# Forget gates and keys as two sigmoids, level products in a fourth bank beside the latent attention, and one accumulator per half for the latents' and heads' output projection

## The reference

```
for l in range(2):
    h = x @ w_in[l]            # hg_q, hg_f, hg_i, hg_gate (1024 each), mla_cq, mla_ckv, mla_kr, mla_gate, mem_q, mem_gate
    # recurrent heads (8 heads of 128)
    logf = log_sigmoid(hg_f) + log1p(lb * exp(-hg_f))      # f = lb + (1 - lb) * sigmoid(hg_f)
    k    = (1 - lb) * sigmoid(-hg_f)
    S_t  = diag(f_t) S_{t-1} + k_t v_t^T ;  o_t = S_t^T q_t         # v = hg_i
    y_hg = rmsnorm_per_head(o) * out_g * silu(hg_gate)
    # latent attention (8 heads of 64 + 32), causal softmax
    y_mla = attend(...) * silu(mla_gate)
    # memory attention (4 heads of 128)
    y_mem = attend(...) * silu(mem_gate)
    x = layernorm(4 ** 0.25 * x + concat(y_hg, y_mla, y_mem) @ w_out[l])
```

## Time and profile before

| | us |
|---|---|
| runs (3): lowest, median, highest | 1034.55, 1035.75, 1036.23 |
| the profiled execution: its time | 1040.25 |
| the profiled execution: its span | 1038.5 |
| TensorE busy in the span | 997.3 |
| VectorE busy | 690.4 |
| ScalarE busy | 605.7 |
| mean granted clock of TensorE | 0.980 |

### The profile page before, as it was taken

How to read it: one execution, slowest core, us unless ns; L and a number is a source line. 1 busy time by engine, 2 the same in 40 slices (tenths; PEclk the granted TensorE clock), 3 DMA queues, 4 the chain that set the end, 5 groups by cost and what they waited for, 6 DMA issues and landing times.

```text
span 1038.5 us, 18803 instructions
## 1 busy us (share of the span) xinstructions
PE 997.3 (96%) x8042; PEld 896.5 (86%) x8042; DVE 690.4 (66%) x917; ACT 605.7 (58%) x828; POOL 10.8 (1%) x14
## 2 busy tenths in 40 slices
PE   9999999999999999999999999896999999998967
PEld 7899887888989999988999998695799999977945
DVE  5775588875656887865565646983675556579645
ACT  7687567554465666554466768347355666682561
POOL 0000000000000000000000000100000000010000
PEclk9999999999999999999999999998999999998989
DMA  8852455477557556666554534434455555234411
GB/s 291 279 172 82 143 171 167 132 232 206 180 148 239 168 173 193 194 213 184 166 163 131 183 103 142 144 111 135 144 176 152 152 150 178 80 123 153 155 61 40
DMA packets 97283, 166.45 MB, mean 160 GB/s; under 512 B 6896, under 2 KB 32240, under 8 KB 96816
## 3 DMA queue, kind: packets, MB, share of 16 engines
q1 hardware_dynamic: 95792, 159.18, 48.8%
q0 software_dynamic: 976, 4.46, 1.3%
q10 hardware_dynamic: 432, 1.62, 0.4%
HBM read 164.19 MB, written 1.05 MB: 159 GB/s over the span
## 4 chain that ended last, share of the span: by engine, by line
PE 90%; ACT 4%; issue 3%; DVE 3%; DMA 1%; SPq 0%; DVEq 0%; ACTq 0%
PE proj L625 13%; PE proj L616 13%; PE proj L626 13%; PE proj L627 13%; PE proj L617 13%; PE proj L618 13%; PE mix L951 1%; PE mix L661 1%; PE mix L686 1%; PE mix L669 1%; ACT whi L1064 1%; PE mix L886 1%; DVE arena L1932 1%; DMA raw<-in_w_mem_kv 1%; PE mix L694 1%
## 5 line engine op out<-in xcount | busy, mean ns | idle before, releaser
L1526 DVE TENSOR_TENSOR wlo<-raw,whi 128x1024 fp32r<-128x1024 f32 (+2 forms) x304 | 355.2, 1198 | 162.1 <-ACT whi L1064 160.6
L1064 ACT ACTIVATE whi<-raw 128x1024 fp32r<-128x1024 f32 (+2 forms) x304 | 306.6, 1038 | 207.7 <-PE proj L627 90.5
L616 PE MATMUL proj<-act_hi,whi 128*128 128x256 f32 x1064 | 304.8, 287 | 2.8 <-ACT arena L1081 2.2
L617 PE MATMUL proj<-act_lo,whi 128*128 128x256 f32 x1064 | 301.7, 284 | 0.0
L618 PE MATMUL proj<-act_hi,wlo 128*128 128x256 f32 x1064 | 301.6, 284 | 0.0
L616 PEld LDWEIGHTS proj<-act_hi,whi 128*128 128x128 f32 x1064 | 203.9, 192 | 5.7 <-ACT arena L1081 3.1
L617 PEld LDWEIGHTS proj<-act_lo,whi 128*128 128x128 f32 x1064 | 203.9, 192 | 0.5
L618 PEld LDWEIGHTS proj<-act_hi,wlo 128*128 128x128 f32 x1064 | 204.0, 192 | 0.2
L625 PE MATMUL proj<-whi,y_hi 128*128 128x512 f32 (+1 forms) x340 | 138.1, 406 | 19.8 <-DVE X L2041 18.6
L626 PE MATMUL proj<-wlo,y_hi 128*128 128x512 f32 (+1 forms) x340 | 135.3, 398 | 0.0
L627 PE MATMUL proj<-whi,y_lo 128*128 128x512 f32 (+1 forms) x340 | 134.6, 396 | 0.0
(11 more groups left out here) (347 smaller groups left out, 1037.3 us busy)
## 6 DMA issues: line engine op xcount, KB each, us to landing
raw<-in_w_in SPq DMA_DIRECT2D x144, 512.0 KB, 4.5
raw<-in_w_up SPq DMA_DIRECT2D x88, 256.0 KB, 4.4
raw<-in_w_out SPq DMA_DIRECT2D x32, 512.0 KB, 4.6
raw<-in_w_down SPq DMA_DIRECT2D x22, 512.0 KB, 5.4
raw<-in_w_mem_k SPq DMA_DIRECT2D x8, 512.0 KB, 3.8
raw<-in_w_o SPq DMA_DIRECT2D x8, 512.0 KB, 3.9
raw<-in_w_mem_v SPq DMA_DIRECT2D x8, 512.0 KB, 3.5
raw<-in_w_mem_kv SPq DMA_DIRECT2D x7, 512.0 KB, 6.6
```

What stands on the lines that cost most here:

```text
L616: mm(o, wh[:, i, wc], hi[:, k0 + i, :], start=begin and j % 2 == 0, stop=False, skip_group_check=True)
L617: mm(o, wh[:, i, wc], lo[:, k0 + i, :], start=False, stop=False, skip_group_check=True)
L1064: fn(whi[c % SPLIT][:, 0:w], raw[c % SLOTS][:, 0:w], ACT.Copy).then_inc(s.w_hi, 1)
L1526: tt(wlo[c % SPLIT][:, 0:w], raw[c % SLOTS][:, 0:w], f32(whi[c % SPLIT][:, 0:w]), ALU.subtract).then_inc(s.w_lo, 1)
```

## The change

It has three parts. (1) ScalarE takes `FORGET` and `HKT` as sigmoids of hg_f and of -hg_f straight from the projection's bank; VectorE's forget arithmetic goes, the second layer scales in place. The keys and grown queries move to memory under `y_hi` and `y_lo`, `TOTAL` to a tile of its own. (2) The latent scores are packed into three banks of `mix` (`LATENT`), and levels 8 to 5 use the fourth, in turns with the latent attention's steps and with at least one projection piece between levels. (3) The two output projections of latents and heads become `heads0` and `heads1`, each with 6 pieces summed in one accumulator: the latents' two pieces first, then the heads' four. `mlaout0`, `mlaout1`, their two additions to X and `hgo` go; all four output pairs are in `mix`; `squares` writes the bank it read from, after `gated`. ScalarE and not VectorE copies the diagonal.

```diff
-    at = [name for name, _ in groups].index("hgg0")
-    groups[at:] = [("mlaout0", mlaout[0]), ("hgg0", hg["hgg0"]), ("hgg1", hg["hgg1"]), ("mlaout1", mlaout[1]), ("hgo", [])]
-    groups += [(f"hgout{c}", wide(out, c * 512)) for c in range(2)]
+    groups += [(f"heads{c}", wide(out, c * 512, row=1024, rows=512) + wide(out, c * 512)) for c in range(2)]
     if L + 1 < LAYERS:
...
 LEVELS = (8, 7, 6, 5, 4, 3, 2, 1, 0)
-LEVEL_BANK = {8: 1, 7: 2, 6: 3, 5: 0, 4: 1, 3: 2, 2: 3}
+LEVEL_BANK = {8: 3, 7: 3, 6: 3, 5: 3, 4: 2, 3: 1, 2: 3}
 GROWS = 7
 
 
...
-        if key[1] == "hgout0":
-            runs = [((key[0], f"hgout{c}"), b, e) for c, b, e in ((0, 0, 3), (1, 0, 1), (0, 3, 4), (1, 1, 4))]
+        if key[1] == "heads0":
+            runs = [((key[0], f"heads{c}"), b, e) for c, b, e in ((0, 0, 2), (1, 0, 2), (0, 2, 4), (1, 2, 3), (0, 4, 6), (1, 3, 6))]
         elif key[1] == "memq":
             runs = [((key[0], name), b, b + 2) for b in (0, 2) for name in ("memq", "memg")]
-        elif key[1] == "hgi1":
-            runs = [(key, 0, 3), ((key[0], "mlaout0"), 0, 2), (key, 3, 4)]
...
-        HQP = ar(4096, 8, SEQ)
-        TOTAL = {1: FORGET.rearrange("p h t -> p (h t)"), 2: ar(6144, 1024), 4: ar(7168, 512), 8: ar(7680, 256),
-                 16: ar(7936, 128), 32: ar(8064, 64), 64: ar(8128, 32)}
-        HQT, HKT, HV, HGT = ar(14336, 8, SEQ), ar(10240, 8, SEQ), ar(12288, NB, DM), ar(8192, 8, SEQ)
+        HKT, HQP = under_y[:, 0, 0:8, :], under_y[:, 1, 0:8, :]
+        TOTAL = {1: FORGET.rearrange("p h t -> p (h t)"), 2: total[:, 0:1024], 4: total[:, 1024:1536], 8: total[:, 1536:1792],
+                 16: total[:, 1792:1920], 32: total[:, 1920:1984], 64: total[:, 1984:2016]}
+        HQT, HSQ, HV, HGT = ar(14336, 8, SEQ), ar(10240, 8, SEQ), ar(12288, NB, DM), ar(8192, 8, SEQ)
         LNG, LNB = ar(12288, DM), ar(13312, DM)
         C_hi, C_lo = y_hi[:, 8:11, :], y_lo[:, 8:11, :]
         MEM_hi, MEM_lo = y_hi[:, 14:22, :], y_lo[:, 14:22, :]
         def sides(half, four):
...
+        LATENT = mix[:, 0:3, :].rearrange("p n c -> p (n c)").rearrange("p (h t) -> p h t", t=TRI)
...
-                        mm(mix[:, hh, 0:P], q[:, 0:P], k[:, 0:P], start=True, stop=True)
-                        last = mm(mix[:, hh, P:TRI], q[:, P:SEQ], k, start=True, stop=True)
+                        o = LATENT[:, hh, :]
+                        mm(o[:, 0:P], q[:, 0:P], k[:, 0:P], start=True, stop=True)
+                        for cols in ((slice(0, P), slice(P, SEQ)) if hh == 2 else (slice(0, SEQ),)):
+                            last = mm(o[:, P + cols.start:P + cols.stop], q[:, P:SEQ], k[:, cols], start=True, stop=True)
...
+                        if l in (7, 6, 5):
+                            pe.wait_ge(s.hg_cp, 6 * L + 8 - l)
+                        elif l == 2:
+                            pe.wait_ge(s.hg_cp, 6 * L + 4)
+                        elif l == 1:
                             pe.wait_ge(s.mla_g, 2 * L + 2)
-                        elif 1 < l < 5:
...
+                    pe.wait_ge(s.hg_w, 4 * L + p + 1)
+                    mm(mix[:, p, :], ones, pair_of(HSQ, p), start=True, stop=True).then_inc(s.hg_ss, 1)
...
+                def heads_ready(k):
+                    if k > 4:
+                        pe.wait_ge(s.hg_yl, 4 * L + (k - 4) // 2)
+
+                def latent_piece(c, n):
+                    project(f"heads{c}", L, y_hi, y_lo, 8, part=(n, n + 1))
+
+                pe.wait_ge(s.mla_tk, 8 * L + 8)
+                scores(0)
+                project("hgq1", L, act_hi, act_lo)
+                turn_shares(0)
+                piece_of("hgi0", 0)
+                pe.wait_ge(s.mla_ptk, 2 * L + 1)
+                pe.wait_ge(*out_of("uv", L))
+                values(LV, LPT[0], range(0, 4)).then_inc(s.mla_y, 1)
                 products(8)
+                piece_of("hgi0", 1)
+                pe.wait_ge(s.mla_g, 2 * L + 1)
+                scores(1)
                 products(7)
+                piece_of("hgi0", 2)
+                piece_of("hgi0", 3)
                 products(6)
+                piece_of("hgi1", 0)
+                piece_of("hgi1", 1)
+                turn_shares(1)
                 products(5)
+                piece_of("hgi1", 2)
+                pe.wait_ge(s.mla_ptk, 2 * L + 2)
+                values(LV, LPT[1], range(4, 8)).then_inc(s.mla_y, 1)
+                piece_of("hgi1", 3)
                 products(4)
+                piece_of("hgg0", 0)
+                piece_of("hgg0", 1)
                 products(3)
+                piece_of("hgg0", 2)
                 products(2)
+                piece_of("hgg0", 3)
                 products(1)
+                piece_of("hgg1", 0)
+                piece_of("hgg1", 1)
                 products(0)
+                piece_of("hgg1", 2)
                 for half in range(2):
                     pe.wait_ge(*out_of(f"hgi{half}", L))
                 pe.wait_ge(s.hg_at, L + 1)
                 for p in range(4):
+                    outputs(p)
+                piece_of("hgg1", 3)
                 squares(0)
                 squares(1)
+                pe.wait_ge(*stage(4, L))
+                latent_piece(0, 0)
                 squares(2)
                 squares(3)
+                latent_piece(0, 1)
+                latent_piece(1, 0)
+                latent_piece(1, 1)
+                project("heads0", L, y_hi, y_lo, -4, ready=heads_ready, part=(2, 4))
+                project("heads1", L, y_hi, y_lo, -4, part=(2, 3))
+                project("heads0", L, y_hi, y_lo, -4, ready=heads_ready, part=(4, 6))
                 if L + 1 < LAYERS:
+                    project("heads1", L, y_hi, y_lo, -4, part=(3, 6), half=s.tok_half)
                     pe.wait_ge(s.mem2_ok, L + 2)
                     project("memk", L, MEM_hi, MEM_lo)
+                else:
+                    project_by_block("heads1", L, y_hi, y_lo, -4, 3, s.tok_half)
...
+                def forgets(four):
+
+                    name, h = f"hgf{four}", slice(4 * four, 4 * four + 4)
+                    split_until(pieces_until(name, L))
+                    act.wait_ge(*done(name, L))
+                    fn(FORGET[:, h, :], tiles(name, L), ACT.Sigmoid)
+                    fn(HKT[:, h, :], tiles(name, L), ACT.Sigmoid, scale=-1.0).then_inc(out_of(name, L)[0], 1)
+
+                def keys(four):
+
+                    act.wait_ge(s.hg_f, four + 1)
+                    for j in range(4 * four, 4 * four + 4):
+                        fn(HKT[:, j, :], HKT[:, j, :], ACT.Copy, scale=cur[:, 12 + j:13 + j]).then_inc(s.hg_x, 1)
...
+                nc.scalar.preload_act_table(ACT.Sigmoid)
+                forgets(0)
+                for n, dst in enumerate((LQT, LKT)):
+                    for pr in range(4):
+                        act.wait_ge(s.mla_t, 8 * L + 4 * n + pr + 1)
+                        fn(dst[0:QK_D, 2 * pr:2 * pr + 2, :], mix[0:QK_D, pr, :].rearrange("p (h t) -> p h t", h=2), ACT.Copy).then_inc(s.mla_tk, 1)
+                forgets(1)
+                nc.scalar.preload_act_table(ACT.Exp)
+                split_until(ahead_of("hgq1", L, 0))
+                if L:
+                    keys(0)
+                shares(0)
+                split_until(ahead_of("hgq1", L, 1))
+                split_until(ahead_of("hgq1", L, 2))
+                shares_turned(0)
+                leave_only("hgq1", L, HQT[:, 4:8, :])
+                if L:
+                    keys(1)
+                split_until(ahead_of("hgi0", L, 0))
+                latent_out(0)
+                split_until(ahead_of("hgi0", L, 1))
...
+                leave_only("hgg1", L, HGT[:, 4:8, :], ACT.Silu)
+                nc.scalar.preload_act_table(ACT.Ln)
                 logs(0)
                 logs(1)
+                split_until(ahead_of("heads0", L, 1))
+                logs(2)
+                logs(3)
                 roots(0)
+                split_until(ahead_of("heads1", L, 0))
+                roots(2)
                 rounded(0)
                 rounded(1)
+                split_until(ahead_of("heads1", L, 1))
                 rounded(2)
                 rounded(3)
+                for name in ("heads0", "heads1"):
                     split_until(pieces_until(name, L))
 
                 for b in range(NB):
@@ -1898,7 +1884,7 @@
...
+                forgets(0)
+                maxima(0)
+                forgets(1)
+                queries(0)
+                totals(2)
+                shares(0)
+                split_until(ahead_of("hgq1", L, 0))
+                for half in HALVES[4::-1]:
+                    totals(half)
+                split_until(ahead_of("hgq1", L, 1))
+                split_until(ahead_of("hgq1", L, 2))
+                queries(1)
+                latent_gated(0)
+                split_until(ahead_of("hgi0", L, 0))
+                masked(8)
+                latent_lower(0, s.mla_yl)
+                split_until(ahead_of("hgi0", L, 1))
+                maxima(1)
```

(82 more changed lines are left out.)

266 lines of the change are left out of this document (71 added, 195 removed).

## The result

The changed kernel takes 1008.06 us (median of four executions) against 1035.99 us (1034.55 to 1039.01) for the kernel before: ratio 0.9724, 95% interval 0.9696 to 0.9752, or 27.9 us less. Predicted were 1007 us, 998 to 1017.

A forecast was written before the change was run, and what follows sets the result against it. TensorE was taken as the bound, busy 997.3 of 1038.5 us. Gains of 33.6 less losses of 5.6 gave net 28 to 29; 28.5 was taken from the 1035.75 median, giving 1007 us, range 998 to 1017 (8 in 10).

The forecast's parts named there:

- Output pieces: At the output projections, TensorE's 9.3 us wait per layer and two slow-clock stretches behind them go: 22.6 us gained.
- rival B: At the heads' output, the ScalarE and VectorE chain is still late: 1016, or 1030 if the wait stays whole; chance 0.09.
- Rival D: No effect: the output pieces' 9.3 us move to waiting for y_lo, shared-bank waits eat the rest; 1036, chance 0.03.
- The wait at L1081: At `hgg0`, TensorE no longer waits for the eviction of `hgi1`'s bank: 2.2 us gained.
- Copies behind the sigmoids: At the latent query and key transposes, two sigmoids delay ScalarE's copies: 0.9 us lost per layer, 1.8 in all.
- Bank 3: Levels 8 to 5 share a bank and wait for `masked`: 3.0 us lost before level 6, 0.4 before level 5.
- Rival C: In levels 8 to 5, shared-bank waits become a chain no longer covered by projection pieces: slower, 1051; chance 0.03.
- Instructions: In the small products, instruction-fetch waits fall from 9.1 to 2.4 us as pieces separate the levels: 6.7 us gained.
- Clock: In the products, half-clock loss after waits falls from 5.5 to 3.4 us, one stretch per layer: 2.1 us gained.

The follow-up runs named there:

- less-cover run: The changed kernel with two latent pieces moved behind the first two pieces of the heads' output in the second half; 1020.64 us, ratio to the kernel before 0.9855.
- separate sums added early: The changed kernel with separate output groups for latents and heads, the latents' sums added to X around `lower(0)`; 1007.0 us, ratio to before 0.9717.
- copies-first run: The changed kernel with ScalarE copying out transposed latent queries and keys ahead of the first half's two sigmoids; 1005.64 us, ratio to before 0.97.
- shifted run: The changed kernel with eight wide and 39 narrow idle matmuls at the start for ten wide, putting later TensorE instructions 148 places on; 1022.08 us, one execution.
- later-level-6 run: The changed kernel with `products(6)` behind the first piece of `hgi1`, `shares(1)` ahead of level 5's grows and a split behind `masked(6)`; 999.92 us, ratio to before 0.9648.
- levels-apart run: The kernel before with only TensorE's order changed: a latent output piece between levels 8 and 7, a values piece between 7 and 6; 1033.3 us, ratio 0.9979.
- separate sums late: The changed kernel with separate output groups for latents and heads, both additions to X behind `scaled(3)`; 1013.87 us, ratio to before 0.9793.

## Why the prediction was right, step by step

**Output pieces (22.6 forecast).** Right. Nothing is left of 2 x 9.3 us, and the pieces run at the upper level. The reckoning of the chain held nearly to the tenth: `products(0)` ends at 690.4 in layer 0, so the forecast puts the end of `lower(0)` at 714.4 and `heads0` piece 2 at 716.1; measured are 714.2 and 716.05, a margin of 1.8 us where I had 1.6. The less-cover run shows that the margin is real, and rival B (chain late) needed 1.8 us and found none. Rival D falls with it. The shared accumulator has no share of its own in it, as the separate sums added early show; it is one way to free the heads from the addition, and the early addition is another. What the first part of the change (the sigmoids) is worth by itself no run shows: VectorE and ScalarE are busy 15.7 and 16.2 us less, and no wait of TensorE before the change named their forget arithmetic.

**The wait at L1081 (2.2).** Right, gone.

**Copies behind the sigmoids (1.8 lost).** Right. The transposes of a layer run from 591.42 to 596.19, 4.8 us where 4.7 were forecast and 3.9 were needed before, so 0.9 us a layer is lost, 1.8 in all; 1.5 of them are on the list of waits. The copies-first run takes it away again.

**Bank 3 (3.0 + 0.4 lost).** Right: 1.46 and 1.47 us before level 6 against 1.5 forecast, none before level 5. Rival C (a chain of bank waits, 1051) saw no second link.

**Instructions (6.7 gained).** The sum agreed, 9.1 to 2.3 us (forecast 2.4), but by luck, since the places were wrong. I forecast 1.2 us in level 3 of layer 0 and 1.1 in level 8 of layer 1; found is one wait in level 6 of layer 0. The step that failed is "a block that TensorE runs through in under 3.3 us makes it wait for the difference".

Counting TensorE's records (matmuls, weight loads, semaphore instructions) from the start, each instruction wait inside the products stands at a place that leaves 193 or 194 on division by 256 (8641, 9409, 13761 and 14017 before, 8898 now, 14273 in the shifted run). So the block length in the forecast holds. With it the two forecast places can be looked up in the changed kernel. TensorE ran through the block with level 8 of layer 1 in 2.1 us (891.26 to 893.33) and through the one with level 3 of layer 0 in 2.5 us (670.65 to 673.19), and waited behind neither. The instruction queue's packet had started at 889.0 in the first case, ahead of the block, and at 670.7 in the second, as TensorE entered it. My count of places was off too: the levels begin 20 and 22 records into these blocks, where I had 26 and 16.

So what decides is how early the next block is asked for. In the changed kernel TensorE is released for level 6 at 642.6. No queue moves anything from 641 to 643.6; the instruction queue's one packet starts at 643.9, 1.1 us after TensorE starts the level, and work resumes at 646.24, 2.4 us after that. The DMA queues of the changed kernel from 643.6 to 646.3 us (packets, megabytes, share):

```profile
q1 hardware_dynamic: 164, 0.34, 48.8%
q8 instruction: 1, 0.02, 2.1%
```

The same 2.3 to 2.4 us lie between packet and resumption in four stops of the kernel before (653.8 to 656.16, 670.8 to 673.07, 931.2 to 933.59, 935.8 to 938.14, the second of each pair from the earlier trace rows). In the shifted run it is 2.7 us.

Why the request came so late stays open. The level's block begins 13 matmuls before the level does, and one guess is that the request is held while the engine's stream stands at the wait for the bank. Then the 1.46 us of bank wait gave no cover, and the piece ahead of it, which I had counted as 3.8 us of block and safe, gave none either. For the guess: in the shifted run the wait in level 6 of layer 1 stands in the same place of its block and behind the same kind of wait, and in the later-level-6 run the same number of instructions finds the bank free and level 6 has no instruction wait. Against it: TensorE entered the block at 638.2, 3.1 us before it stood still, and no packet came then either. In the kernel before a packet of the instruction queue starts at 999.7 us, in the middle of the 9.3 us in which TensorE stands at the output pieces (997.4 to 1006.7). And in the levels-apart run the two waits that the guess would keep went. The later-level-6 edit took the bank wait and the block's neighbours away at once, so it does not separate them. The packet of 935.8 in the kernel before came 2.2 us after its block had begun, though TensorE waited for no other engine there.

The Trainium skill, Runtime: NRT & Kernel Launch, section Instruction fetch mechanics, calls the crossing of a block's boundary mostly hidden. These runs agree for most boundaries: 63 blocks were fetched, and the list has five waits before and one after. They do not agree inside the small products: 9.1 us before, 7.0 of them in levels 8 and 7, which stand back to back, and 2.3 us after.

**Clock (2.1 gained in the products).** 5.5 us of loss became 5.9 x 0.5 = 2.9; forecast 3.4, as one stretch in each layer. There is one in layer 0, after 1.46 + 2.26 us of standstill, and none in layer 1, after 1.47.

**The sum.** In the profiled executions the spans differ by 33.2 us, not 28.5. Of the 4.7, 1.7 are for a half-clock stretch of 3.4 us at 178 us, in the first block, which the profiled execution of before had and this one has not; 1.2 for the waits behind weights' low parts, which went too and which I did not count; 0.5 each for the clock in the products and for bank 3. The rest, 0.8, I can't assign: the terms also sum to 28.0 or 28.4 and not to the 28.5 that I took, and two profiles can be 0.7 us apart after 36 us without any change there. The median of before lies 4.5 us under its profiled execution, which I subtracted as if it were a constant of measuring. It is the clock: that execution had a mean granted clock of 0.980, while 29 others of the same kernel had 0.982 to 0.989 (1033.9 to 1039.1 us), and 0.005 of 1036 is 5 us. So part of the slow stretches that I counted as gain is not in the median execution. Two errors of the same size, one of each sign: that the forecast of 1007 came out so near is luck. The levels-apart run shows the same: 7.4 us by the spans, 2.2 by the medians.

## What to carry to other kernels

When an engine waits for a buffer that a late addition frees, look for independent work to put between the last producer and the first consumer before redesigning the accumulation: here four pieces of 2.7 us did it, with a shared accumulator or with separate sums added early. Keep long projections between runs of tiny matmuls, and avoid a semaphore wait in front of such a run: it costs its own length, sometimes a late fetch of the next instructions (2.3 us here; that the wait causes it is not shown), and sometimes the clock. And take a sum made against one profiled execution together with that execution's clock: where its mean granted clock differs from that of the other runs, so do the terms.

## What the runs showed of the hardware

- Half clock followed standstills of TensorE of 1.88 us, 2.08, 2.3 (separate sums late, layer 0), 2.55 (shifted), 3.6 (less cover) and 1.46 + 2.26 (changed), and not single ones of 1.44 to 1.73, nor that of 2.3 in layer 1 of the separate sums late. The length of a standstill alone doesn't tell what follows it.
- A busy TensorE can lose its clock as well: under 78 matmuls of 8 columns, back to back and 0.18 us each, it fell to 0.50 though TensorE had not been idle since 1.2 us, and stayed there for 17 us, into the wide matmuls that followed.
- Between the start of an instruction packet and the first matmul that waited for it lay 2.3 to 2.4 us in five stops and 2.7 us in a sixth. A packet can start late (at 643.9, 5.7 us after TensorE entered the block ahead of it) or in good time (at 889.0, 2.2 us before that).
